# An ordered-by-planner middle stage and twice-loaded spectra in a Hyena/mLSTM encoder layer

## What is computed

```python
def hyena_mix(x1, x2, v, kspec, bias):
    def long_conv(z, ks, d):
        zf = jnp.fft.rfft(z, n=2 * L, axis=1)
        return jnp.fft.irfft(zf * ks[None], n=2 * L, axis=1)[:, :L] + d * z
    z = x1 * long_conv(v, kspec[:, 0], bias[0])
    return x2 * long_conv(z, kspec[:, 1], bias[1])

def encoder_layer(x, ...):
    ...                                    # norm, projection, depthwise convolution
    y_hy = hyena_mix(x1, x2, hv, kspec, hy_bias)
    hm = mlstm_bidir(q, k, v, gates)       # forward and backward state over chunks
    ...
    x = x + jnp.concatenate([y_hy, y_ml], axis=-1) @ w_out
    ...                                    # norm, gated MLP, residual
```

## Time and profile before

| | |
|---|---|
| median of 3 runs | 2239.07 us (2234.37 to 2241.76) |
| profiled execution, its own time | 2236.85 us |
| its span in the profile | 2235.0 us |
| first stage | to 726 us of the span |
| middle stage, up to the first product of the third | 726 to 1092 us |
| third stage | from 1092 us |

### The profile page before, as it was taken

How to read it: one execution, slowest core, us unless ns; L and a number is a source line. 1 busy time by engine, 2 the same in 40 slices (tenths; PEclk the granted TensorE clock), 3 DMA queues, 4 the chain that set the end, 5 groups by cost and what they waited for, 6 DMA issues and landing times. The chain is left out here.

```text
span 2235.0 us, 26984 instructions
## 1 busy us (share of the span) xinstructions
PE 2139.8 (96%) x9878; PEld 1775.1 (79%) x9878; DVE 1517.8 (68%) x2078; ACT 934.1 (42%) x1482; POOL 379.4 (17%) x350
## 2 busy tenths in 40 slices
PE   6999999999999899898799999999999999999998
PEld 5788878887877788787688878888888888888886
DVE  6577677555754378577546876569999999655554
ACT  5432233325543445455325543344444444442342
POOL 0221122100110101000000056312353433100000
PEclk9999999999999899899999999999999999999999
DMA  4344444553663866758735278633334443866553
GB/s 152 109 141 139 130 130 131 160 155 133 207 195 118 256 182 208 217 166 236 254 111 191 99 257 302 220 116 107 132 137 141 141 137 104 270 232 195 172 161 118
DMA packets 239164, 377.93 MB, mean 169 GB/s; under 512 B 17816, under 2 KB 143384, under 8 KB 239034
## 3 DMA queue, kind: packets, MB, share of 16 engines
q1 hardware_dynamic: 217802, 300.70, 43.6%
q0 software_dynamic: 19936, 72.10, 8.7%
q10 hardware_dynamic: 1296, 3.41, 0.4%
HBM read 252.08 MB, written 98.11 MB: 157 GB/s over the span
## 5 line engine op out<-in xcount | busy, mean ns | idle before, releaser
L128 PE MATMUL in_acc<-in_h_hi,in_w_hi 128*128 128x512 f32 x464 | 191.0, 412 | 2.6 <-DVE in_h_lo L1175 2.6
L130 PE MATMUL in_acc<-in_h_hi,in_w_lo 128*128 128x512 f32 x464 | 182.0, 392 | 0.0
L129 PE MATMUL in_acc<-in_h_lo,in_w_hi 128*128 128x512 f32 x464 | 181.5, 391 | 0.0
L128 PE MATMUL mlp_bank<-down_d_hi,down_s_hi 128*128 128x512 f32 x462 | 179.7, 389 | 0.0
L129 PE MATMUL mlp_bank<-down_d_lo,down_s_hi 128*128 128x512 f32 x462 | 179.7, 389 | 0.0
L130 PE MATMUL mlp_bank<-down_d_hi,down_s_lo 128*128 128x512 f32 x462 | 179.7, 389 | 0.0
L1057 ACT ACTIVATE in_w_hi<-in_w_raw 128x1024 fp32r<-128x1024 f32 x58 | 61.5, 1060 | 214.5 <-PE in_acc L130 214.3
L128 PE MATMUL mlp_bank<-mlp_s_hi,up_w_hi 128*128 128x512 f32 x352 | 138.8, 394 | 3.1 <-DVE up_w_lo L2956 3.1
L129 PE MATMUL mlp_bank<-mlp_s_lo,up_w_hi 128*128 128x512 f32 x352 | 138.2, 393 | 0.0
L130 PE MATMUL mlp_bank<-mlp_s_hi,up_w_lo 128*128 128x512 f32 x352 | 138.0, 392 | 0.0
L2882 ACT ACTIVATE down_s_hi<-down_s_raw 128x1408 fp32r<-128x1408 f32 x42 | 58.0, 1382 | 167.2 <-PE mlp_bank L130 167.2
(11 more groups left out here) (298 smaller groups left out, 5522.4 us busy)
## 6 DMA issues: line engine op xcount, KB each, us to landing
in_w_raw<-arg_w_in_t SPq DMA_DIRECT2D x58, 512.0 KB, 3.6
down_s_raw<-s_scratch SPq DMA_DIRECT2D x42, 704.0 KB, 4.5
up_w_raw<-arg_w_up_t SPq DMA_DIRECT2D x44, 512.0 KB, 3.6
wide_raw<-arg_w_up_t SPq DMA_DIRECT2D x44, 512.0 KB, 3.7
filt_tab<-arg_fwd SPq DMA_DIRECT2D x32, 512.0 KB, 3.8
mix_classes<-mix_split SPq DMA_DIRECT2D x48, 256.0 KB, 8.9
mix_kf<-k_scratch SPq DMA_DIRECT2D x48, 256.0 KB, 4.4
mix_split<-mix_classes SPq DMA_DIRECT2D x48, 256.0 KB, 5.2
```

Source lines behind the costliest of these rows:

```text
L128: pe.matmul(out, w_hi, x_hi, start=first, stop=False, skip_group_check=joins)
L129: pe.matmul(out, w_hi, x_lo, start=False, stop=False, skip_group_check=joins)
L130: return pe.matmul(out, w_lo, x_hi, start=False, stop=last, skip_group_check=joins)
```

## The change

- The hand-written order of the middle stage goes. `plan` makes it from streams of steps for every engine, SyncE's DMA issues and GpSimd's mask additions included, each with a time and a delay. A DMA is modelled as a step of SP: 0.72 us for 256 KB, and 3.5 to 5 us until it has landed. `takes` lets the planner count PSUM banks, and `rank_of` breaks ties between steps that could start at once by how far the convolutions and the heads have come.
- The turns run in another order: streams 2 and 3 first, and the pairs of (1,0) are cut in two, four before (0,1) and four after it, ahead of (1,1). Storage changes with it (`slot`): stream 0 shares its tiles with nobody's convolution before it, stream 1 takes those of 2 and 3.
- Each spectrum is loaded twice: whole into `kf`, and in two DMAs of 64 partitions (128 KB each) with exchanged halves into `kf_turned`. The second product of a pair is then one operation over 128 partitions.
- The output weights' load waits for the store of stream 0 (before: of streams 2 and 3).

```diff
+    runs = [(0, 2, 0, n_pairs[2]), (0, 3, 0, n_pairs[3]), (0, 0, 0, n_pairs[0]), (1, 2, 0, n_pairs[2]), (1, 3, 0, n_pairs[3]),
+            (1, 0, 0, early), (0, 1, 0, n_pairs[1]), (1, 0, early, n_pairs[0]), (1, 1, 0, n_pairs[1])]
...
+        if kind == "shuffle":
+            o, st, b = a
+            return "SP", 0.72, 3.5, [("copy_split",) + a] + ([last_block("back", 0, st)] if o else [("store", 2), ("store", 3)] if st == 1 else [])
+        if kind == "load_k":
+            return "SP", 1.44, 3.5, [("multiply", a[0] - ring)] if a[0] >= ring else []
+        if kind == "forward":
+            o, st, t = pairs[a[0]]
+            return "PE", 0.87, 0.1, [last_block("shuffle", o, st), ("load_k", a[0])] + ([("inverse", a[0] - lag)] if a[0] >= lag else [])
+        if kind == "multiply":
+            return "DVE", 1.45, 0.1, [("forward", a[0]), ("load_k", a[0])] + ([("inverse", a[0] - 2)] if a[0] >= 2 else [])
+        if kind == "inverse":
+            return "PE", 1.74, 0.1, [("multiply", a[0])]
...
+        if kind == "back":
+            o, st, b = a
+            return "SP", 0.72, 3.5, [("copy_classes", g) for g, x in enumerate(pairs) if x[:2] == (o, st)]
+        if kind == "join":
+            return "PE", 0.87, 0.1, [("back",) + a, ("load_gate",) + a[:2]]
...
+        if kind == "store":
+            return "ACT", 0.2, 5.0, [last_block("copy_turned", a[0])]
...
+        if kind == "load_head":
+            j = a[0]
+            return "SP", 6.8 * size, 4.0, [last_tile("attend", j - 2)] if j >= 2 else []
...
+        if kind == "load_wo":
+            return "SP", 1.4, 4.0, [("store", 0), ("forward", len(pairs) - 4)]
...
+    def rank_of(n, at, step):
+        conv = step[0] in conv_kinds
+        if work(step)[0] == "SP":
+            return 0.0 if conv else 1.0
+        some = range(len(conv_streams)) if conv else range(len(conv_streams), len(costs))
+        share = sum(costs[i][at[i]] for i in some) / sum(costs[i][-1] for i in some)
+        return share + 0.05 if conv else share
...
+    order = plan(conv_streams + head_streams + [
...
+        by_turn("shuffle", split_turns), [("load_k", g) for g in all_pairs], by_turn("back", turns),
...
+        [("load_wo", n) for n in range(KD)], [("load_so", b) for b in range(2)]], work, rank_of=rank_of, takes=takes)
...
         def slot(st):
-            return (0, 0) if st < 2 else (1, (st - 2) * big // 2)
+            return (1, 0) if st == 0 else (0, 0 if st == 1 else (st - 2) * big // 2)
...
                 def load_k(g):
...
-                    sp.dma_start(kf[g % ring][:, :, :], k_d[s][o, t, half, :, :, :]).then_inc(k_loaded[g % ring], 16)
+                    if g >= ring:
+                        sp.wait_ge(sem["multiplied"], g - ring + 1)
+                    for to, rows, of in ((kf, slice(0, P), slice(0, P)), (kf_turned, slice(0, SUB), slice(SUB, P)), (kf_turned, slice(SUB, P), slice(0, SUB))):
+                        sp.dma_start(to[g % ring][rows, :, :], k_d[s][o, t, half, of, :, :]).then_inc(k_loaded[g % ring], 16)
...
                     dve.tensor_tensor(prod[g % 2][:, :, 0, :], x[:, :, :], kk[:, :, :], ALU.mult)
-                    dve.tensor_tensor(prod[g % 2][0:SUB, :, 1, :], x[0:SUB, :, :], kk[SUB:P, :, :], ALU.mult)
-                    dve.tensor_tensor(prod[g % 2][SUB:P, :, 1, :], x[SUB:P, :, :], kk[0:SUB, :, :],
-                                      ALU.mult).then_inc(sem["multiplied"], 1)
+                    dve.tensor_tensor(prod[g % 2][:, :, 1, :], x[:, :, :], kf_turned[g % ring][:, :, :], ALU.mult).then_inc(sem["multiplied"], 1)
```

More of the change, by code:

```diff
@@ L362, with plan @@
               [N_KINDS - 1] + MIX_V_O + list(range(N_QK))]
-def plan(streams, work, even=False):
-    clock, done, order, at = {}, {}, [], [0] * len(streams)
+def plan(streams, work, even=False, rank_of=None, takes=None, banks=8):
+    clock, done, order, at, held = {}, {}, [], [0] * len(streams), []
     while True:
@@ L1428, in outwards @@
         return [x for i in range(nt // 2) for x in (nt // 2 - 1 - i, nt // 2 + i)]
[L1430 to L1500, removed]
@@ L1528, in long_convolutions_and_heads, with tiles_of, quads_of, last_link @@
-    schedule += [(x[0],) + x[2:] for x in heads[at:]]
-    for n, step in enumerate(schedule):
-        if step[0] == "load":
-            near = [m for m in range(n, min(n + 12, len(schedule))) if schedule[m][0] == "back"]
-            if near:
-                schedule.insert(near[-1], schedule.pop(n))
-                break
+    def tiles_of(j):
+        return range(nts[jobs[j][1]])
+    def quads_of(j):
+        return range(nts[jobs[j][1]] // quad)
+    def last_link(j):
+        return ("add_state", j, len(tiles_of(j)) - 2)
@@ new lines, in takes, with by_turn, by_tile @@
+    def takes(step):
+        kind, a = step[0], step[1:]
+        release = {"split": ["copy_split"], "forward": ["multiply"], "inverse": ["copy_classes"], "join": ["finish"], "turn": ["copy_turned"],
+                   "keys": ["scale_keys", "weigh"], "link": ["add_state"], "attend": ["combine", "combine"], "turn_head": ["scale"]}
+        return [(x,) + a for x in release.get(kind, [])]
+    def by_turn(kind, some):
+        return [(kind, o, st, b) for o, st in some for b in blocks(st)]
+    def by_tile(kind, count=0):
+        return [(kind, j, i) for j in all_jobs for i in tiles_of(j)[:len(tiles_of(j)) - count]]
@@ new lines, in by_quad @@
+    def by_quad(kind):
+        return [(kind, j, i) for j in all_jobs for i in quads_of(j)]
+    all_pairs = range(len(pairs))
+    split_turns = [(0, 2), (0, 3), (0, 0), (1, 2), (1, 3), (1, 0), (0, 1), (1, 1)]
+    split_turns = sorted(split_turns, key=lambda x: pair_at[x + (0,)])
+    outer_turns = [st for o, st in turns if o]
+    conv_streams = [by_turn("join", turns), [("turn", st, b) for st in outer_turns for b in blocks(st)], by_turn("split", split_turns),
+                    [("inverse", g) for g in all_pairs], [("forward", g) for g in all_pairs]]
@@ new lines, in long_convolutions_and_heads @@
+    conv_kinds = ("join", "turn", "split", "inverse", "forward", "multiply", "finish", "copy_split", "copy_classes", "copy_turned", "store",
+                  "shuffle", "load_k", "back", "load_gate", "load_z", "load_wo", "load_so")
+    def rank_of(n, at, step):
[5 more added lines that the diff above has]
+        return share + 0.05 if conv else share
@@ L1544, in take @@
         vy.append(release)
-    for step in schedule:
+    for step in order:
         kind, args = step[0], step[1:]
```

240 lines of the change are left out of this document (133 added, 107 removed).

## The result

| | before | after |
|---|---|---|
| median, both kernels in turn on one chip (20 runs each) | 2240.49 us | 2246.31 us |
| ratio, 95% interval | | 1.0035 [1.0026, 1.0045] |
| span of the profiled execution | 2235.0 us | 2242.3 us |
| first product of the middle stage to first of the third | 365.8 us | 377.4 us |
| third stage | 1142.8 us | 1139.2 us |

The change makes the kernel slower by 0.35%, some 8 us; forecast was a gain of 21 us. The whole loss lies in the middle stage: it is 11.6 us longer, and the rest of the profiled execution 4.3 us shorter.

The account below looks back on a forecast made before the run. TensorE bounds the outer stages; gains lie in the middle stage's idle time and clock loss. Work 291, idle 37 and clock 17 give 345 us against 366, a gain of 21: 2218 us, likeliest 2200 to 2232, eight in ten 2190 to 2256.

Parts of the forecast that it names:

- the order: Middle stage: the planned order removes 36 us of TensorE's inner stalls, with 18 us of late-transfer waits in their place.
- the start, the border and the drain: Middle stage: idle time no order removes, at its start, the third-stage border and the last turn's drain; 19 us in all.
- the price of the second load: Middle stage: 12.6 MB more on the DMA engines, 32 to 63 us of added DMA time.
- lateness at 16 places of turns: Eight turns, a shuffle and a `back` each, land later than planned: 1.1 us each on average, 18 us.
- the middle price: Middle-stage DMA busy time with the second load, taken as 311 us, the middle of 296 to 327.
- my lower bound: Second load priced at the 390 GB/s of row loads: 0.67 us a pair, 32 us in all.
- The products: VectorE loses 33.4 us of middle-stage work; nothing counted, at most 0.7 us a pair where an inverse directly follows its product.
- The late transfers: Middle-stage waits where transfers land later than the plan's clock assumes: 18 us, mostly at first forwards and joins of turns.
- The ratio of clock loss to idle time: Middle stage: each idle TensorE microsecond costs 0.46 us of clock loss; 17 us in the forecast.
- The signs of being wrong: Forecast wrong if TensorE's middle-stage idle time is under 25 or over 51 us, or the third-stage border grows.
- idle time only moves: Rival, 16%: the 16 late places cost 2.0 us each, middle-stage idle time stays 51 us, time 2239 us.
- DMA engines become the bound: Rival, 20%: the second load at its upper price, 327 us of DMA time, makes the middle stage 385 us; 2258 us.

Follow-up runs that it names:

- experiment 4: The change with planner ties broken by the longest chain of work behind a step; ratio 1.0012 to the kernel before.
- experiment 3: The change with the second spectrum copy loaded by one DMA over 128 partitions, halves not exchanged (wrong data); ratio 0.9962 to the kernel before.
- experiment 5: The change with the real half stored twice, so one DMA over 128 partitions loads the exchanged copy with right data; ratio 0.9964 to the kernel before.
- experiment 1: The change's order alone: each spectrum loaded once and multiplied in three operations; ratio 1.0042 to the kernel before.
- experiment 9: The kernel before, hand-written order, with two products and the exchanged copy loaded by one DMA over 128 partitions; ratio 0.9986 to the kernel before.
- experiment 2: The kernel before, hand-written order, with the change's two-operation products and doubled loads (two half-wide DMAs); ratio 1.0055 to the kernel before.
- experiment 7: The kernel before, hand-written order and three products, with the exchanged halves loaded by half-wide DMAs but never read; ratio 1.0098 to the kernel before.
- experiment 14: Experiment 1 without spectrum loads after the third pair (later products use wrong spectra); ratio 1.0014 to the kernel before.
- experiment 13: The change without spectrum loads after the third pair (later products use wrong spectra); ratio 0.9884 to the kernel before, 2217.04 us.
- experiment 12: Experiment 5 with DMA prices measured in the traces given to the planner, the change's ties kept; ratio 0.9974 to the kernel before, 2234.7 us.
- experiment 11: Experiment 6 with the change's own DMA prices in the planner; ratio 0.9966 to the kernel before, 2232.6 us.
- experiment 6: Experiment 5 with longest-chain ties, measured DMA prices, `lag` 3 and `early` 3; ratio 0.9863 to the kernel before, 2209.58 us, fastest of all.

## Why the prediction was wrong

**The step that failed first** is that of the order: "The plan places each of these steps only when its needs are met by its own clock, so I take them as gone". I took 36 us of inner stalls out and put in only 18 us for late transfers and nothing for waits of the plan's own: idle time 37 us. Measured are 61.3 us. The stalls that I named did mostly go, but meeting a need by the clock doesn't mean that TensorE is busy until then: the plan's own clock holds 49.3 us of idle time, 16.5 of them at 13 inverses put right behind their product, and the chip waits at 13 places too, for 18.1 us. This could have been counted ahead of any run. It is the tie-break that does it and not every list scheduler: with the longest chain and the same lag the plan has 3 such places and the chip 3 (experiment 4). The forecast missed by 29 us (a gain of 21, a loss of 8). With a wide copy the change gains 8 us, so 13 of the 29 are left when the price of the halves is taken off.

How the 61.3 us part is read from the table of waits: 18.1 on products, of which some 13.5 are VectorE's pace (13.6 and 13.4 in experiments 3 and 5) and the rest late spectra; 7.0 for ScalarE's copies; 23.7 for late joins, the tile loaded again and stream 1's forward; 7.9 for the border; some 4 at steps of the heads. Where I had 19 us for the start, the border and the drain, the start cost nothing, and the drain shows only as a late join of 4.9 us. That the 7.0 us comes from ScalarE's queue is read from one timeline and wasn't taken away by itself.

**The second step that failed** is the price of the second load, which my sum gave no term beside lateness at 16 places of turns. As two half-wide DMAs it costs 22 us in the written order even unread, and 15, 16 and 20 us more than one wide DMA of the same bytes in the three orders of the table. That makes the other 16 of the 29 us. It isn't only that a pair waits for its spectrum: between the change and experiment 3 product waits are 4.5 of the 10 us of idle time. DMA time came out as forecast, 309 us for 311, but the middle price didn't hold elsewhere. Against the same order with a single load (0.68 x 384.6 = 262 us in experiment 1, 264) the wide copy adds 30 us in both (experiments 3 and 9), 0.62 us a pair, a little under my lower bound of 0.67. The halves add 48 us in the order of the change and 58 in the written one (experiment 2, 0.84 x 382.7). The shares are rounded, so each of these is good to some 4 us. The rule that I weighed (the Trainium skill, SBUF — State Buffer, "Can I just issue two DMAs to hit both halves?") agrees in its direction, since the two DMAs take 1.6 times the DMA time of the wide one in the change's order, 1.9 times in the written one, for the same bytes. SyncE's side was mis-sized as well: I counted 96 issues of 0.32 us, 31 us, and they took 0.69 each, 66 us; the queue's wait for multiplied pairs, its room, fell from 113.7 to 50.5 us. How much of the 16 us is the width and how much the issues stays open.

**The products.** "I count nothing for it" doesn't hold: the saved operation is worth 10 us in the written order (experiments 7 and 2) and 29 us in the planned one, between experiments 14 and 13. I had the condition ("an inverse directly behind its product") and its price, "at most 0.7 us a pair", 33.4 us in all, and didn't ask how often the planned order meets it. The product waits are 15.7 us shorter (27.5 to 11.8), other waits some 4 us, among them 2.7 for ScalarE's copy; the clock's part falls from 379.8 - 291 - 58.3 = 30.5 to 347.3 - 291 - 38.5 = 17.8 us. Without loads and with three operations the order costs 3 + 18 = 21 us against the written one.

**The late transfers** were sized about right: joins 13.1 us, stream 1's tile 6.7, stream 1's forward 3.9, together 23.7 for 18. But they weren't where I put them: shuffles landed in 5.1 us, earlier than before, and of the turns' first forwards only stream 1's shows such a wait. Joins waited for 2.2 us on average (13.1 over 6), which my marker read as "the plan's landing times are the failed step". Experiment 12 speaks against it: with landing times from the trace and the ties of the change nothing is won. Under the longest chain the same prices give 23 us (11 to 6), so they matter for an order, but they aren't what made the change slow.

**The ratio of clock loss to idle time** held: 0.41 where I took 0.46 from before; over the runs it goes from 0.37 (experiment 7) to 0.52 (experiment 14), so it is a rough price. **The border** grew by 0.7 us, which is nothing. **The signs of being wrong** worked: idle time came out over 51 us. One bound was mis-added: by my own terms 2200 us stands for 0.3 us a place, and 0.6 gives 2206.

**The rivals.** Of mine, "idle time only moves" came nearest (2239 us), and the mechanism is in part its own: idle time moved to places of another kind. "DMA engines become the bound" had the sign right, with too high a price (2258 us): at a share of 0.82 over the stage they aren't the bound, though they are in stretches (1.06 from 741 to 765), and the loss comes by waits. My marker for it was badly put, since a low share can as well come from a stage that is long for another cause.

**What adds up.** Along one way of the table, with three operations first: the order costs 9 us, the two operations with a wide copy give 17 back (+9 to -8), and the copy's two halves take 16: +8 us. Along another: the two operations with a wide copy give 3 in the written order, the order of the change 5 more, and the halves take 16. What the order is worth depends on the operations that it runs with; the 16 us of the halves are there both ways.

**What stays open.** Why the measured prices give 23 us under the longest chain and nothing under the ties of the change. Experiments 6 and 11 also have a lag of 3 and `early` at 3, experiment 12 has 2 and 4, so a part may lie there; that wasn't told apart. What can be read is that experiment 11 waits 13.5 us at the border and experiment 4 waits 15.5 us at a spectrum, and experiment 6 has 8.8 us at the border and no such stall at a spectrum.

## What to carry to other kernels

Before trusting a list scheduler, run it alone and add up the idle time on its own clock: here it showed 49.3 us and 13 consumers directly behind their producer on another engine, and another tie-break had 3. An operation that costs little under a hand-written order can be the critical one there. Load an exchanged copy with one DMA over all 128 partitions, even at the price of storing half of it twice: same bytes loaded, 15 to 20 us of 2240. Price an added transfer by who waits for it and by what stands behind its issues, and not by the busy share of the DMA engines alone. The planner's clock tells where it leaves holes; it doesn't rank schedules, so compare those on the chip.

## What the hardware showed beside that

- Half as many bytes landed no sooner: 5.2 us for a 128 KB load over 64 partitions, and 5.2 and 5.0 us for 256 KB over 128 in the same place of the queue (experiments 3 and 5), medians.
- With the DMA engines saturated, an issue itself holds up SyncE: 7.5 us for one DMA of 256 KB at 762 in experiment 4, share 1.07, where a spectrum load's issue takes 0.32 us elsewhere.
- Loads that nobody reads, and that leave the DMA engines idle for nearly a fifth of the stage, cost 22 us, in part by the clock, 0.91 against 0.94 in the earlier trace rows.
